# Four edits around the setup and layer 0's output stages of a two-block transformer kernel

## What is computed

```python
def first_block(x, c, ctx, c_ctx, w_mod, b_mod, w_in, ...):
    xl, xc = x, ctx
    for l in range(DEPTH):
        sh_l, sc_l, g_l = jnp.split(jax.nn.silu(c) @ w_mod[l] + b_mod[l], 3, axis=-1)
        sh_c, sc_c, g_c = jnp.split(jax.nn.silu(c_ctx) @ w_mod[l] + b_mod[l], 3, axis=-1)
        hl = xl * (1.0 + sc_l[:, None, :]) + sh_l[:, None, :]
        hc = xc * (1.0 + sc_c) + sh_c
        parts_l = jnp.split(hl @ w_in[l], SPLIT_POINTS, axis=-1)
        ...
        out_l = _mix_output(parts_l, att_l, ...)
        xl_new = _layernorm(DEEPNORM_ALPHA * xl + g_l[:, None, :] * out_l, ln_g[l], ln_b[l])
        if not last:
            out_c = _mix_output(parts_c, att_c, ...)
            xc = _layernorm(DEEPNORM_ALPHA * xc + g_c * out_c, ln_g[l], ln_b[l])
        xl = xl_new
    return xl
```

## Time and profile before

| | |
|---|---|
| three runs | 3285.61, 3285.64, 3286.28 us |
| profiled execution, its own time | 3285.07 us |
| its span in the trace | 3283.2 us |
| TensorE (PE) busy | 3187.1 us, 97% |
| PE weight loads | 2612.6 us, 80% |
| VectorE (DVE) | 2240.6 us, 68% |
| ScalarE (ACT) | 1344.8 us, 41% |
| GpSimd (POOL) | 293.7 us, 9% |
| chain of waits, share of PE | 83% |
| mean granted clock | 0.989 |

### The profile page before, as it was taken

How to read it: one execution, slowest core, us unless ns; L and a number is a source line. 1 busy time by engine, 2 the same in 40 slices (tenths; PEclk the granted TensorE clock), 3 DMA queues, 4 the chain that set the end, 5 groups by cost and what they waited for, 6 DMA issues and landing times.

```text
span 3283.2 us, 47624 instructions
## 1 busy us (share of the span) xinstructions
PE 3187.1 (97%) x16736; PEld 2612.6 (80%) x16736; DVE 2240.6 (68%) x3570; ACT 1344.8 (41%) x2077; POOL 293.7 (9%) x522
## 2 busy tenths in 40 slices
PE   7999999999999999999999999999998999999997
PEld 3699999888777777879888777777786888788786
DVE  3388768765677775687656677774777899655446
ACT  2335564432444445137422444444326323454423
POOL 0000002001011010110101010000112000000001
PEclk8999999999999999999999999999999999999998
DMA  9775557556454443655755444432563332222333
GB/s 400 254 235 201 200 187 284 195 192 232 152 163 144 161 136 130 240 192 174 252 201 197 149 159 138 150 129 80 186 218 135 129 102 90 97 86 87 103 115 103
DMA packets 111661, 556.42 MB, mean 169 GB/s; under 512 B 17936, under 2 KB 22080, under 8 KB 68512
## 3 DMA queue, kind: packets, MB, share of 16 engines
q1 hardware_dynamic: 51424, 348.15, 29.9%
q0 software_dynamic: 60096, 206.39, 19.0%
HBM read 531.33 MB, written 23.09 MB: 169 GB/s over the span
## 4 chain that ended last, share of the span: by engine, by line
PE 83%; DVE 7%; DMA 3%; ACT 2%; issue 2%; DVEq 2%; ACTq 0%; POOL 0%; POOLq 0%; SPq 0%
PE acc L1426 23%; PE acc L1428 23%; PE acc L1427 23%; PE pv L1608 3%; PE S L1582 2%; DMA gates<-in_wm 2%; DVE w_lo L1997 2%; PE S L1597 1%; DVE gates L2050 1%; DMA xy<-in_wm 1%; PE misc L1514 1%; PE misc L1619 1%; ACT w_hi L736 1%; PE acc L1450 1%; ACT work L736 1%
## 5 line engine op out<-in xcount | busy, mean ns | idle before, releaser
L1426 PE MATMUL acc<-h_hi,w_hi 128*128 128x512 f32 (+1 forms) x4448 | 1624.4, 365 | 17.2 <-DVE w_lo L1997 12.7
L1428 PE MATMUL acc<-h_hi,w_lo 128*128 128x512 f32 (+1 forms) x4448 | 1593.8, 358 | 0.0
L1427 PE MATMUL acc<-h_lo,w_hi 128*128 128x512 f32 (+1 forms) x4448 | 1592.4, 358 | 0.0
L1426 PEld LDWEIGHTS acc<-h_hi,w_hi 128*128 128x128 f32 x4448 | 841.8, 189 | 167.5 <-issue 38.7
L1427 PEld LDWEIGHTS acc<-h_lo,w_hi 128*128 128x128 f32 x4448 | 842.4, 189 | 124.4 <-issue 6.7
L1428 PEld LDWEIGHTS acc<-h_hi,w_lo 128*128 128x128 f32 x4448 | 841.6, 189 | 124.4
L1997 DVE TENSOR_TENSOR w_lo<-raw,w_hi 128x1024 fp32r<-128x1024 f32 x584 | 689.2, 1220 | 193.5 <-ACT w_hi L736 189.8
L736 ACT ACTIVATE w_hi<-raw 128x1024 fp32r<-128x1024 f32 x584 | 585.5, 1053 | 83.6 <-PE acc L1481 31.1
L736 ACT ACTIVATE ev<-acc 128x512 f32<-128x512 f32 (+1 forms) x202 | 106.5, 532 | 809.0 <-PE acc L1428 797.1
L539 POOL DMA_DIRECT2D gates<-in_wm x288 | 153.0, 531 | 1407.6 <-DVE gates L2050 1234.0
L736 ACT ACTIVATE work<-S,small 128x768 f32<-128x768 f32 (+1 forms) x160 | 129.0, 813 | 258.7 <-DVE small L2166 258.7
(11 more groups left out here) (307 smaller groups left out, 2684.7 us busy)
## 6 DMA issues: line engine op xcount, KB each, us to landing
raw<-in_w SPq DMA_DIRECT2D x288, 1024.0 KB, 5.0
gates<-in_wm POOLq DMA_DIRECT2D x288, 512.0 KB, 4.7
xy<-in_wm SPq DMA_DIRECT2D x32, 1024.0 KB, 8.1
raw<-in_wp SPq DMA_DIRECT2D x4, 1024.0 KB, 14.9
x_d<-xy POOLq DMA_DIRECT2D x1, 4096.0 KB, 15.4
qb<-x_d POOLq DMA_DIRECT2D x16, 256.0 KB, 4.0
kb<-x_d POOLq DMA_DIRECT2D x16, 256.0 KB, 4.6
bias_d<-kb POOLq DMA_DIRECT2D x8, 384.0 KB, 20.8
```

Of the source, the lines that this page charges most:

```text
L1426: mm(o, w_hi[:, w], h_hi[:, x], start=n == 0, stop=False)
L1427: mm(o, w_hi[:, w], h_lo[:, x], start=False, stop=False)
L1428: last = mm(o, w_lo[:, w], h_hi[:, x], start=False, stop=n == len(ks) - 1)
```

## The change

- SyncE's order of setup: the first quarter of the pooling weights goes ahead of everything; ctx comes from SyncE's queue by quarters of 512 KB, each behind x's quarter and in its semaphore; the other loads stand one to three steps later.
- TensorE: the bias row's product stands behind step 1; early blocks begin with step 4 (`FIRST_EARLY`); the first two tiles of cconv are done one after the other (`first_context_tiles`).
- ScalarE empties `acc` when step 28 is done, ahead of the last `mod0_row`, and does `context_quarter(2)` ahead of `hi` of the second tile; VectorE does `context_quarter(2)` ahead of `mod0_add(7)` and `context_quarter(3)` ahead of `lo`, with the memsets last.
- ScalarE does `squared` ahead of `hi` in cpool's last tile.
- GpSimd asks for cout's first modulation tile ahead of its wait for cpool, and for `c_row(1)` and aout's first two modulation tiles when the last scores of the heads are done, which TensorE signals (`s_ready`).

```diff
@@ -473,10 +473,12 @@
                 if q >= 2:
                     sp.wait_ge(e_lo, shown(e_lo, 4 * (q - 1)))
                 sp.dma_start(x_quarters[q % 2], A["xT"][:, 4 * q:4 * (q + 1)]).then_inc(x0_landed[q % 2], 16)
-
-            EARLY_LOADS = {3: 0, 6: 1, 11: 2, 16: 3}
+                sp.dma_start(work[:, 4 * q * CTX:4 * (q + 1) * CTX].rearrange("p (k t) -> p k t", t=CTX),
+                             A["ctxT"][:, 4 * q:4 * (q + 1)]).then_inc(x0_landed[q % 2], 16)
+
+            EARLY_LOADS = {0: 0, 7: 1, 12: 2, 17: 3}
             EARLY_X = {4: 0, 8: 1, 13: 2, 18: 3}
-            FIRST_LOADS = {24: 0, 26: 1}
+            FIRST_LOADS = {25: 0, 29: 1}
             for e in range(M0_STEPS):
                 if e in EARLY_LOADS:
                     q = EARLY_LOADS[e]
@@ -596,9 +598,11 @@
 
                 T = TOK.get(c, SEQ)
 
-                def body(i):
+                def body(i, begun=False):
                     for p in range(4):
-                        if phase == "cout":
+                        if begun and p == 0:
+                            pass
+                        elif phase == "cout":
                             mods(phase, 0, cout_mods(i, p))
                         elif phase in CHUNK0:
                             mods(phase, i, range(2 * p, 2 * p + 2))
@@ -614,7 +618,10 @@
                                 pool.dma_start(late_x(k), A["xT"][:, k]).then_inc(x_land, 16)
                 if phase == "cout":
                     for i in range(4):
-                        body(i)
+                        body(i, begun=i == 0)
+                elif phase == "aout":
+                    body(0, begun=True)
+                    loop(pool, 1, 4, body)
                 else:
                     loop(pool, 0, 4, body)
 
@@ -631,9 +638,8 @@
                              (bias_row[:], A["negmask"])):
                 pool.dma_start(dst, src).then_inc(consts, 16)
 
-            for dst, src in ((edge[:], A["edge"]),
-                             (work[:, 0:KT * CTX].rearrange("p (k t) -> p k t", t=CTX), A["ctxT"])):
-                pool.dma_start(dst, src).then_inc(late_consts, 16)
+            pool.dma_start(edge[:], A["edge"]).then_inc(late_consts, 16)
+
             def c_row(v):
                 for h in range(2):
                     row = csil_d[v:v + 1, P // 2 * h:P // 2 * (h + 1), :].rearrange("o p k -> (o p k)")
@@ -655,6 +661,7 @@
             pool.wait_ge(y_pre, shown(y_pre, 8))
             pool.dma_start(y_pool_d, u_padded(True)[:, :, PAD:PAD + SEQ]).then_inc(y_pool_st, 16)
             pool.wait_ge(y_pool_st, shown(y_pool_st, 16))
+            mods("cout", 0, cout_mods(0, 0))
             pool.wait_ge(dve_phase, shown(dve_phase, after("cpool")))
             residual("c", "cout", A["ctxT"])
 
@@ -666,8 +673,9 @@
             pool.dma_start(xy3[:, 12:KT], y_pool_d).then_inc(y_pool_ld, 16)
             pool.wait_ge(dve_phase, shown(dve_phase, after("aconv")))
             head_step("a")
-            pool.wait_ge(dve_phase, shown(dve_phase, after("ahead")))
+            pool.wait_ge(s_ready, shown(s_ready, N0["a"] + 4 * N_HEADS))
             c_row(1)
+            mods("aout", 0, range(0, 2))
             pool.wait_ge(dve_phase, shown(dve_phase, after("apool")))
             pool.wait_ge(x_st, shown(x_st, 16))
             pool.dma_start(work[:, 0:KT * CTX].rearrange("p (k t) -> p k t", t=CTX), c1_d).then_inc(x_land, 16)
@@ -872,13 +880,14 @@
 
                     i = N_HEADS
                     for p in range(4):
+                        if p == 3:
+                            squared(i, last_osq)
                         hi(j_at("cpool", 0, p + 1))
                         if p < QT:
                             exps(i, p)
                         if p == 0:
                             inverse_root(i)
                         if p == 3:
-                            squared(i, last_osq)
                             for n in range(8, 11):
                                 y_high(c, n)
                             inverse_root(i + 1)
@@ -1111,7 +1120,7 @@
             def early_high(q):
 
                 act.wait_ge(m0_mod, shown(m0_mod, q + 1))
-                act.wait_ge(x0_landed[q % 2], shown(x0_landed[q % 2], 16 * (q // 2 + 1)))
+                act.wait_ge(x0_landed[q % 2], shown(x0_landed[q % 2], 32 * (q // 2 + 1)))
                 if q >= 2:
                     act.wait_ge(tile_done, shown(tile_done, q - 1))
                 x_place, ctx_place = early_place(q)
@@ -1129,7 +1138,6 @@
                     modulate_pair("c.h", ctx_tile, CTX, *by_set(1), i)
 
             hi(At(0))
-            act.wait_ge(late_consts, shown(late_consts, 32))
             mod0_row(0)
             early_high(0)
             mod0_row(1)
@@ -1147,14 +1155,14 @@
             context_quarter(0)
             mod0_row(6)
             context_quarter(1)
-            mod0_row(7)
             act.wait_ge(u_ctx_ready, shown(u_ctx_ready, 1))
-            act.wait_ge(m0_used, shown(m0_used, M0_STEPS))
+            act.wait_ge(m0_used, shown(m0_used, M0_STEPS - M0_SLOTS + 1))
             for n in range(2):
                 f(u_padded(False)[:, 2 * n:2 * n + 2, PAD:PAD + CTX],
                   acc[n][:, :].rearrange("p (g t) -> p g t", t=CTX)).then_inc(u_evac, 1)
+            mod0_row(7)
+            context_quarter(2)
             hi(j_at("cconv", 0, 1))
-            context_quarter(2)
             context_quarter(3)
             act.wait_ge(tile_done, shown(tile_done, EARLY))
             for g in range(4):
@@ -1455,13 +1463,13 @@
                 if k == KT - 1:
                     last.then_inc(tile_done, 1)
 
-            def first_context_blocks(k):
+            def first_context_tiles():
 
                 o = (acc[0][:, 0:CTX], acc[1][:, 0:CTX])
-                if k == 0:
-                    pe.wait_ge(u_evac, shown(u_evac, 2))
+                pe.wait_ge(u_evac, shown(u_evac, 2))
                 for t in range(2):
-                    pair_block(o, j_at("cconv", 0, 0), H_AT["c.h"], t, k)
+                    for k in range(KT):
+                        pair_block(o, j_at("cconv", 0, 0), H_AT["c.h"], t, k)
 
             def early_block(q, t, n, of_x):
 
@@ -1819,13 +1827,13 @@
 
             early = [(q, t, n, of_x) for q in range(3) for t in range(4) for n in range(4) for of_x in (True, False)]
             early += [(3, t, n, of_x) for of_x in (False, True) for t in range(4) for n in range(4)]
-            FIRST_EARLY, KEPT = 6, 5
+            FIRST_EARLY, KEPT = 4, 5
             at = 0
             for e in range(M0_STEPS):
                 if e and e % 4 == 0:
                     mod0_transposes(e // 4 - 1)
                 mod0_step(e, e % M0_SLOTS)
-                if e == M0_SLOTS:
+                if e == 1:
                     pe.wait_ge(consts, shown(consts, 6 * 16))
                     mm(S[0:16, 3 * SEQ:3 * SEQ + 384], ev[3][0:32, 0:16], ev[3][0:32, 16:400], start=True, stop=True)\
                         .then_inc(setup_pe, 1)
@@ -1839,8 +1847,7 @@
             for b in early[at:]:
                 early_block(*b)
             mod0_transposes(M0_GROUPS - 1)
-            for k in range(KT):
-                first_context_blocks(k)
+            first_context_tiles()
             for c in "cab":
                 conv(c)
                 if c == "c":
@@ -2692,7 +2699,7 @@
             dve.wait_ge(setup_pe, shown(setup_pe, 1))
             tt(bias_row[:], bias_row[:], S[0:16, 3 * SEQ:3 * SEQ + 384], ALU.add).then_inc(setup_dve, 1)
             lo(At(0))
-            dve.wait_ge(late_consts, shown(late_consts, 32))
+            dve.wait_ge(late_consts, shown(late_consts, 16))
             mod0_add(0)
             early_low(0)
             mod0_add(1)
@@ -2710,15 +2717,15 @@
             context_quarter(0)
             mod0_add(6)
             context_quarter(1)
+            context_quarter(2)
             mod0_add(7)
             phase_done("setup")
+            context_quarter(3)
+            lo(j_at("cconv", 0, 1))
             for is_x in (False, True):
                 u = u_padded(is_x)
                 nc.vector.memset(u[:, :, 0:PAD], 0.0)
                 nc.vector.memset(u[:, :, PAD + (SEQ if is_x else CTX):], 0.0)
-            lo(j_at("cconv", 0, 1))
-            context_quarter(2)
-            context_quarter(3)
             for c, l in (("c", 0), ("a", 0), ("b", 1)):
                 T = TOK[c]
                 if c == "a":
```

## The result

| kernel | median, lowest to highest, us | before, same chip | ratio, 95% interval |
|---|---|---|---|
| changed | 3267.43 (3266.48 to 3267.99) | 3285.96 | 0.9944 [0.9932, 0.9956] |
| changed, once more (e12) | 3267.66 (3264.62 to 3268.17) | 3284.47 | 0.9944 [0.9931, 0.9958] |

Forecast 3263, range 3257 to 3271. The change is worth 18.5 us by the medians and 16.8 by the spans of the two profiled executions (3283.2 to 3266.4; its own time is 3267.99), where the forecast had 22.6. The direction and the range held; two terms of the sum did not, and 3267.4 lies just outside the 3259 to 3267 that the forecast gave itself without its rivals.

What follows compares the result with a forecast made beforehand. Setup was taken as bound by transfers before the first block and by PE behind it. Terms -10.1 (start), -2.9, 0, -1.4 and -8.2 sum to -22.6 us from the 3283.2 span, giving a median of 3263 us, range 3257 to 3271.

Steps and rivals of the forecast that it cites:

- First block: Start of setup: first early block at 27.7 us instead of 38.87, 11.2 us earlier.
- the two steps back: Start of setup: steps 5 and 6 now stand behind the first block, 1.06 us each, giving 2.1 us back.
- the two ScalarE stalls: Setup behind the first block: PE's stalls of 0.59 and 1.46 us for ScalarE go, 2.05 us won.
- Waiting for pieces: Start of setup: PE waits about 1 us for step 18's piece; the queue runs ahead after it.
- End of setup: cconv's second and third tiles: PE's stalls of 1.82 and 1.06 us go, -2.9 us, bounds -1.2 and -3.2.
- a new wait of PE in cconv: Sign in cconv, behind setup, that would show the forecast wrong; no size given.
- cpool 0: cpool: the 1.77 us stall goes but PE waits for later work instead, 0 us; bounds +0.4 and -1.77.
- cout -1.4: cout: earlier modulation tile removes PE's 1.55 us wait at the third tile; -1.4 us, bounds 0 and -2.
- aout -8.2: aout's third tile: 5.7 to 6.1 of the 6.14 us stall and 2.2 us of low clock go; bounds -4, -8.4.
- Transfers bind all of setup: Rival in setup: pieces late at each step, start gives 5 to 7 us, not 10; 3267 us, chance 0.17.
- The stall at aout moves to the residual row: Rival at aout: residual row lands at 1310, PE still waits 3 us, clock still falls; 3268 us, chance 0.12.
- setup at half clock: Slower rival: small PE gaps at every step keep setup's clock at 1.2 GHz; up to 3315 us, chance 0.02.

Runs made afterwards that it cites:

- e12: The changed kernel itself, unaltered, run once more beside the version with both moves on the same chip: 3267.66 us, ratio 0.9944 to the kernel before.
- e7: Changed kernel with the first early block behind step 6 instead of step 4: 3271.59 us, ratio 0.9964 to the kernel before.
- e8: Changed kernel with the bias row's product between steps 4 and 5 again: 3271.48 us, ratio 0.9961 to the kernel before.
- e9: Changed kernel with ctx loaded whole at the start from GpSimd's queue, as before: 3269.41 us, ratio 0.9955 to the kernel before.
- e6: Changed kernel with VectorE splitting cconv's second tile ahead of the last quarter of ctx: 3266.50 us, ratio 0.9942 to the kernel before.
- e4: Changed kernel with `squared` behind `hi` again in cpool's last tile: 3266.51 us, ratio 0.9941 to the kernel before.
- e10: Changed kernel with setup loads not needed yet one to three steps later in SyncE's order: 3263.39 us, ratio 0.9939 to the kernel before.
- e2: Changed kernel with aout's first two modulation tiles behind the ctx read again, c row still early: 3271.35 us, ratio 0.9959 to the kernel before.
- e1: Changed kernel with both early requests at aout (c row, modulation tiles) undone: 3274.95 us, ratio 0.9969 to the kernel before.

## Why the prediction was right or wrong

- **First block** (11.2 us forecast, 10.9 measured), the two steps back, the two ScalarE stalls: right. e7 and e8 show what each rests on. What e7, e8 and e9 lose (4.85, 5.0 and 1.1 us) is more together than the 8.8, so the moves lean on each other and none has a share of its own. Of two that make the first block early, the bias row (5.0 us in e8) is a far larger lever than ctx by quarters (1.1 in e9).
- **Waiting for pieces: the step that failed at the start.** The forecast wrote "about 1 us of waiting", 1.0 at step 18, and the row says 1.01 there. That it fits so well is luck: PE was ready at 80.05 us, forecast 78.3, and the piece landed at 81.06, forecast 79.3. Above all it compared the two sums of bytes and of work at step 18 alone, and 1.40 and 0.70 us were lost at steps 8 and 13 before. The bound is not the sum since the start; it is what stands in the queue when a slot comes free, against four steps of work. The rate of the transfers was not what failed: 419 to 422 GB/s from 20 to 80 us. The rule on the page "DMA: Bandwidth & Descriptors" of the Trainium skill, section "Where 436 GB/s comes from", that HBM limits such transfers to about 358 GB/s a core, does not describe this stretch; the same section also has 425 GB/s for a transfer of 16 MB, and the rows are near that. About 1 us came back in the low clock behind the first block, which lasted 1.6 us (27.93 to 29.5) instead of 4.1 (38.87 to 43); that term was not in the sum.
- **End of setup: the second step that failed, -2.9 forecast, -1.15 measured (-0.9 in the mean of ten profiles).** Both stalls that it names went. What failed is "The third tile's 1.06 us go too: ScalarE and VectorE split it while the second runs" as the end of the matter: it did not ask what VectorE's later `lo` does to the raw place, to SyncE's next request, and so to the tiles behind. VectorE freed the place 7.1 us after the transposes (141.04), and before 3.9 us after. e6 shows it. The reason that the forecast gives for the third tile is also only half of it: in the earlier trace rows PE waits there for `ev`, ScalarE's copy out of `acc`, which was made at 157.57 behind the second half of `hi`; in the changed kernel the copy of the first tile is made at 142.06, while PE is at the second. And the forecast names a new wait of PE in cconv as a sign of being wrong; it came, three times.
- **cpool 0**: right, and for its reason (e4).
- **cout -1.4**: 1.95 in the one profile, 0.4 to 1.1 by all. Right in mechanism at the third tile, too high in size.
- **aout -8.2**: 7.8 measured, right in all its parts: 5.8 of the stall, 2.0 of the clock. PE comes to the third tile 10.4 us earlier than before (1298.67 without its wait, against 1309.06); with these, the request at 1261.0 and VectorE's residual at 1296.25 stand for 1271.4 and 1306.6 in the forecast's time, which had 1272 and 1306.9.
- **Sum**: 8.8 + 1.15 + 0 + 1.95 + 5.8 + 2.0 = 19.7, and the spans differ by 16.8. The 3 us between are two periods of low clock, at 637 and 2480 us, in the profile after and not in that of before.
- **The rivals.** "Transfers bind all of setup" gave 3267, close to what came, but for another reason: the start was worth 8.8 us, not 5 to 7, and e10 shows that order binds and not rate. That the median came out at this rival's number is luck. "The stall at aout moves to the residual row" did not happen: the row ends VectorE's wait at 1296.25, early enough for PE, and e2's stall of 3.35 us comes from the modulation tile. The slower side, setup at half clock, did not: behind each of the waits of 0.7 to 1.4 us the products took their 1.06 us for a step, the time of the full clock. The loop on the page "TensorE: Matmul & The Clock Gate", section "HAM oscillation — how this bites in real kernels", of the Trainium skill runs at the low clock because its waits for pieces are longer than the work between them; here the waits were at most a tenth of the work, and the trace agrees in that no low clock came. That a wait must be so long is not shown: the next but one section has periods of low clock behind single waits of 1.20 us.

## What to carry to other kernels

Where pieces go through a few slots, check the transfers at every piece and not at one: what stands in the queue when the slot comes free, against the work of as many steps as there are slots. Load what is not needed yet behind the pieces, not in front (here 1.9 us, e10). And an engine that is given a new order frees its buffers at new times: follow each to the request that waits for it (here 1.1 to 2.0 us for one line, e6).

## What the runs showed of the hardware

**Periods of low clock fall at the same places, but not in every run.** The granted clock falls to 0.50 for 3.4 us, or two or three times that, behind waits of PE. Behind the wait of 1.20 us at 458 us, it does so in six of the thirteen profiles of the changed kernel and its variants (and in that of before), and in seven not. The window in the changed kernel and in e1:

```profile
458.50:463.50 5.00, 5.00 (x27) 4.67 (x28) 4.19 (x9) 2.64 (x6) 0.00 (x0) 0.66 0.49 146
```

```profile
458.90:463.90 5.00, 5.00 (x39) 4.67 (x40) 4.19 (x9) 2.68 (x6) 0.00 (x0) 1.00 0.50 152
```

From the second mark to the third it is 29.52 to 29.56 us in the six and 28.03 to 28.05 in the seven: one period costs 1.5 us. Periods that come and go at a few such places (458, 637, 684 and 2480 us) would account for the spread of 3.5 us in the runs of one kernel; only the profiled runs can show them. What decides whether a period falls is open.

**The record of the clock can be off at the start.** In the changed kernel it reads 1.00 from 20 us on, while step 4 at 26.06 took 1.94 us, as at 0.50 in the earlier trace rows, and later steps 1.06. There the durations tell the clock, and the row does not.
